# Modulation products of a two-block transformer kernel: from TensorE to accumulators on VectorE

## The reference

```python
cond_x = jax.nn.silu(c)
cond_c = jax.nn.silu(c_ctx)[None]
for i in range(DEPTH):
    sx1, cx1, gx1, sx2, cx2, gx2 = jnp.split((cond_x @ ada_w[i] + ada_b[i])[:, None, :], N_MOD, axis=-1)
    sc1, cc1, gc1, sc2, cc2, gc2 = jnp.split((cond_c @ ada_w[i] + ada_b[i])[:, None, :], N_MOD, axis=-1)
    hx = _modulate(_rms(x, norm_mix_g[i]), sx1, cx1)
    # layer 0: x = x + gx1 * mixer(hx), and the same for ctx with sc1, cc1, gc1
    # layer 1: attention; of the context only hc (sc1, cc1) is used
    x = x + gx2 * _mlp(_modulate(_rms(x, norm_mlp_g[i]), sx2, cx2), mlp_w1[i], mlp_w2[i])
    if not last:
        ctx = ctx + gc2 * _mlp(_modulate(_rms(ctx, norm_mlp_g[i]), sc2, cc2), mlp_w1[i], mlp_w2[i])
```

## Time and profile before

| | |
|---|---|
| median of three runs | 2355.6 us |
| the profiled execution, its own time | 2361.12 us |
| its span | 2359.3 us |
| TensorE busy | 2206.5 us, 94% |
| VectorE, ScalarE, GpSimd busy | 962.2, 786.0, 672.8 us |
| mean granted TensorE clock | 0.961 of full speed |
| moved by DMA | 199.92 MB |

### The profile page before, as it was taken

One profiled execution on the slowest core, in us unless ns is written; L12 is line 12 of the kernel. 1 busy time (PEld: TensorE's weight loads), 2 busy tenths in 40 slices (PEclk: granted clock), 3 DMA queues, 4 the chain that ended last, 5 costly groups with the idle time before them and its releaser, 6 DMA issues.

```text
span 2359.3 us, 33158 instructions
## 1 busy us (share of the span) xinstructions
PE 2206.5 (94%) x13714; PEld 1866.6 (79%) x13714; DVE 962.2 (41%) x1322; ACT 786.0 (33%) x1267; POOL 672.8 (29%) x314
## 2 busy tenths in 40 slices
PE   5999989999999998999899999999999896999987
PEld 3777877888888886789787788888898685977766
DVE  3223243222222225653592522222789324066662
ACT  2212223121221213432583422322323533255542
POOL 0321313222222221323495344444020123300002
PEclk9999989999999999999899999999999797999998
DMA  7443214213222231221223232323222010211111
GB/s 272 145 147 141 70 45 170 90 58 139 107 107 92 73 121 36 81 61 60 43 26 99 82 98 89 97 91 97 72 81 73 10 52 30 81 54 55 55 45 45
DMA packets 74313, 199.92 MB, mean 85 GB/s; under 512 B 24656, under 2 KB 25936, under 8 KB 74192
## 3 DMA queue, kind: packets, MB, share of 16 engines
q1 hardware_dynamic: 73008, 197.58, 25.8%
q10 hardware_dynamic: 1184, 0.61, 0.1%
HBM read 194.49 MB, written 2.10 MB: 83 GB/s over the span
## 4 chain that ended last, share of the span: by engine, by line
PE 86%; DVE 5%; POOL 3%; ACT 2%; issue 2%; DMA 1%; SPq 0%; DVEq 0%; ACTq 0%; POOLq 0%
PE ps L1990 60%; PE ps L2111 5%; PE ps L2471 5%; PE ps L2005 3%; POOL NAP L856 2%; PE ps L2040 2%; PE ps L2015 1%; PE ps L2029 1%; PE ps L2175 1%; PE ps L2093 1%; PE ps L2495 1%; PE ps L2022 1%; DVE S L1412 1%; DVE UC L1697 1%; POOL S L826 1%
## 5 line engine op out<-in xcount | busy, mean ns | idle before, releaser
L809 POOL TENSOR_TENSOR WL<-raw,WH 128x1024 fp32r<-128x1024 f32 x215 | 521.3, 2428 | 1390.8 <-ACT WH L906 1390.6
L906 ACT ACTIVATE WH<-raw 128x1024 fp32r<-128x1024 f32 x260 | 273.2, 1054 | 501.4 <-PE ps L1990 481.7
L1990 PE MATMUL ps<-HH,WH 128*128 128x512 f32 (+2 forms) x1568 | 428.1, 340 | 2.5 <-DVE HL L1799 2.5
L1990 PE MATMUL ps<-HL,WH 128*128 128x512 f32 (+2 forms) x1568 | 419.7, 334 | 0.0
L1990 PE MATMUL ps<-HH,WL 128*128 128x512 f32 (+2 forms) x1568 | 419.5, 334 | 0.0
L1990 PEld LDWEIGHTS ps<-HH,WH 128*128 128x128 f32 x1568 | 252.9, 189 | 62.3 <-issue 30.1
L1990 PEld LDWEIGHTS ps<-HL,WH 128*128 128x128 f32 x1568 | 252.2, 189 | 32.0 <-issue 1.4
L1990 PEld LDWEIGHTS ps<-HH,WL 128*128 128x128 f32 x1568 | 252.2, 189 | 31.2
L1990 PE MATMUL ps<-GH,WH 128*128 128x512 f32 (+1 forms) x896 | 267.9, 357 | 3.0 <-issue 3.0
L1990 PE MATMUL ps<-GL,WH 128*128 128x512 f32 (+1 forms) x896 | 268.1, 358 | 0.0
L1990 PE MATMUL ps<-GH,WL 128*128 128x512 f32 (+1 forms) x896 | 266.9, 356 | 0.0
(11 more groups left out here) (263 smaller groups left out, 3321.5 us busy)
## 6 DMA issues: line engine op xcount, KB each, us to landing
raw<-stream SPq DMA_DIRECT2D x260, 512.0 KB, 3.6
ring<-stream SPq DMA_DIRECT2D x40, 1024.0 KB, 4.9
ADA<-stream SPq DMA_DIRECT2D x4, 2048.0 KB, 20.3
XT<-rpb SPq DMA_DIRECT2D x128, 24.0 KB, 2.4
XT<-xT SPq DMA_DIRECT2D x1, 2048.0 KB, 8.7
out<-XT SPq DMA_DIRECT2D x8, 256.0 KB, 2.0
V1s<-V SPq DMA_DIRECT2D x6, 256.0 KB, 4.5
XT<-ctxT SPq DMA_DIRECT2D x1, 1024.0 KB, 11.3
```

The source lines that it names most:

```text
L809: nc.gpsimd.tensor_tensor(WL[:, slot, :], raw[:, slot, :], WH[:, slot, :].bitcast(F32), ALU.subtract).then_inc(lo_done[slot], 1)
L906: nc.scalar.activation(WH[:, slot, :], raw[:, slot, :], ACT.Copy).then_inc(hi_done[slot], 1)
L1990: ins = nc.tensor.matmul(pair(g)[:, cols], lhs, x[:, k, cols], start=first, stop=last)
```

## The change

The 20 later quads are computed on VectorE. Each weight tile is loaded alone (512 KB) into one of two slots (`tile_in`), 80 loads in place of 40. For each of its two blocks of inputs VectorE multiplies the 128 x 512 block with a per-partition scalar, the condition's value for that input, and adds it to an accumulator in SBUF (`ada_products`): two products a block in layer 0 and in the first four quads of layer 1 (`x` and the context), one in the other quads of layer 1, whose context modulation nobody reads. That is 256 products. Four accumulators of 512 columns are a batch. When a batch is complete, TensorE sums it over the partitions (`ada_sums`: two halves of four matmuls of 256 columns with `first`, 32 columns of which one is ones), VectorE copies the sums (`sums_out`), TensorE turns them (`ada_turn`, two halves of two narrow matmuls with `sel4`), and VectorE adds the bias (`ada_cols`). There are four batches in each layer: in layer 0 behind in1 4 and 11, after the first group of dft1, and behind out1 5; in layer 1 behind the second down projection of every other chunk; the turns stand one or two projections later. The two constants widen the constant table by 36 columns; `silu_c` and a clearing of `mod[1]` are new at the start.

```diff
+IN1_ADA = {1: 2, 2: 2, 3: 2, 4: 2, 5: 1, 6: 2, 7: 2, 8: 1, 9: 2, 11: 1, 12: 2, 13: 3, 14: 1, 15: 1}
+IN1_SUMS, IN1_TURNS = {4: 0, 11: 1}, {5: 0, 12: 1}
+    first = [(("in1", i), 0) for i, n in IN1_ADA.items() for _ in range(n)] + [(("out1", m), 0) for m in range(4) for _ in range(2)]
+    return first + [(("up", 0, c, i), c) for c in range(CHUNKS) for i in range(4) for _ in range(1 + c % 2)]
...
@@ SyncE
+            def load_weights(n):
+                if n == 0:
+                    sp.wait_ge(ada_rowed, 4)
+                if n >= 2:
+                    sp.wait_ge(acc_step, ada_tile(n - 1)[5])
+                if n == ADA_IN1:
+                    g = GROUP["dft1", 5]
+                    sp.wait_ge(ps_full[g % 4], turn(g) + 1)
+                layer, quad, kk = ada_tile(n)[0:3]
+                sp.dma_start(ada_ring(n), stream[TILE["ada", layer, 4 * quad + kk]]).then_inc(tile_in[n % 2], 16)
...
                 load_tile(n)
-                while pairs < len(ADA_PAIRS) and ADA_PAIRS[pairs][0] + 3 <= n:
+                while taken < len(ADA_TILES) and TILE[ADA_TILES[taken][0]] + 4 <= n:
+                    load_weights(taken)
...
@@ VectorE
+            nc.vector.tensor_tensor(silu_c[:], sig_c[:], v("cond"), ALU.mult).then_inc(silu_done, 1)
+            nc.vector.memset(mod[1][:], 0.0).then_inc(mod_zero, 1)
...
+            def ada_products(n, q=None):
+                layer, quad, kk, both, to, step = ada_tile(n)
+                count = 16 * (n // 2 + 1)
+                dve.wait_ge(tile_in[n % 2], count if q is None else count + 16 * 6 * q)
+                for k in (2 * kk, 2 * kk + 1):
+                    w = ada_ring(n)[:, 512 * (k % 2):512 * (k % 2) + 512]
+                    for x in range(1 + both):
+                        acc = (ada_acc0, ada_acc1)[n >= ADA_IN1][:, to + x, :]
+                        by = silu_c[:, 2 * k + x:2 * k + x + 1]
+                        if k == 0:
+                            ins = nc.vector.tensor_scalar(acc, w, by, None, ALU.mult)
+                        else:
+                            earlier = step - both
+                            dve.wait_ge(acc_step, earlier if q is None else earlier + 32 * q)
+                            ins = nc.vector.scalar_tensor_tensor(acc, w, by, acc, ALU.mult, ALU.add)
+                        ins.then_inc(acc_step, 1)
+                        step += 1
...
                     x_update(GROUP[kind, m], m, layer, 2, n, order=order)
+                    products_beside((kind, m))
+                    if kind == "out1" and m == 5:
+                        sums_out(0, 3)
+                    if kind == "out1" and m == 6:
+                        ada_cols(0, 3)
...
+                if i in IN1_TURNS:
+                    ada_cols(0, IN1_TURNS[i])
+                if i == 1:
+                    dve.wait_ge(silu_done, 1)
+                products_beside(("in1", i))
+                if i in (4, 10):
+                    sums_out(0, i // 10)
...
+                if t == 0:
+                    sums_out(0, 2)
...
+                        for j in range(1 + c % 2):
+                            ada_products(chunk_ada(c) + (1 + c % 2) * i + j, q)
...
@@ TensorE
-                    for quad, kk in ada_after_up(layer, c, i):
-                        if kk % 2:
-                            ada_pair(1, quad, kk // 2, q)
...
+            def ada_sums(layer, b, q=None):
+                steps = 32 * (b + 1) + 4 * ADA_0 * layer
+                acc = (ada_acc0, ada_acc1)[layer or b == 3]
+                for h in range(2):
+                    g = GROUP["adas", layer, b, h]
                     empty(g, q, MLP_G[0])
+                    pe.wait_ge(acc_step, steps if q is None else steps + 32 * q)
+                    for s in range(4):
+                        ins = nc.tensor.matmul(pair(g)[32 * s:32 * s + 32, 0:256], c_("first"), acc[:, s, 256 * h:256 * h + 256],
+                                               start=True, stop=True)
+                    ins.then_inc(ps_full[g % 4], 1)
...
+            def ada_turn(layer, b, q=None):
+                for h in range(2):
+                    g, rows = GROUP["adat", layer, b, h], GROUP["adas", layer, b, h]
                     empty(g, q, MLP_G[0])
+                    pe.wait_ge(ps_free[rows % 4], turn(rows, q, MLP_G[0]) + 1)
+                    for x in range(2):
+                        ins = nc.tensor.matmul(pair(g)[:, 4 * x:4 * x + 4], ada_rows[:, (2 * h + x) * P:(2 * h + x + 1) * P], c_("sel4"),
                                                start=True, stop=True)
...
+                    if layer == 0 and c % 2 == 0 and m == 1:
+                        ada_sums(1, c // 2, q)
+                    if layer == 0 and c % 2 == 0 and m == 3:
+                        ada_turn(1, c // 2, q)
```

More of the change, by code:

```diff
@@ L168, in norm, with sums, turns @@
         g(("norm", r))
+    def sums(layer, b):
+        for h in range(2):
+            g(("adas", layer, b, h))
+    def turns(layer, b):
+        for h in range(2):
+            g(("adat", layer, b, h))
     g(("adaf", 0))
@@ L175, in _groups @@
             g(("adaf", 1))
[L176 to L180, removed]
+        if i in IN1_SUMS:
+            sums(0, IN1_SUMS[i])
+        if i in IN1_TURNS:
+            turns(0, IN1_TURNS[i])
     for t in range(6):
         g(("dft1", t))
-    g(("adat", 0, 2))
+        if t == 0:
+            sums(0, 2)
+    turns(0, 2)
     for j in range(4):
@@ L187, in _groups @@
         g(("out1", m))
+        if m == 5:
+            sums(0, 3)
+        if m == 6:
+            turns(0, 3)
     def up(layer, c):
@@ L198, in down @@
             g(("down", layer, c, m))
-            if layer == 0 and c % 2 == 0 and m == ADA_TURN:
-                g(("adat", 1, c // 2))
+            if layer == 0 and c % 2 == 0 and m == 1:
+                sums(1, c // 2)
+            if layer == 0 and c % 2 == 0 and m == 3:
+                turns(1, c // 2)
     def mlp(layer):
@@ new lines, in products_beside, with sums_out @@
+            def products_beside(tile):
+                for n in range(ADA_0):
+                    if ADA_TILES[n][0] == tile:
+                        ada_products(n)
+            def sums_out(layer, b, q=None):
+                for h in range(2):
+                    g = GROUP["adas", layer, b, h]
+                    full(g, q, MLP_G[0])
+                    nc.vector.tensor_scalar(ada_rows[:, 256 * h:256 * h + 256], pair(g)[:, 0:256], 1.0, None, ALU.mult)\
+                      .then_inc(ps_free[g % 4], 1)
@@ L1608, in mlp_down @@
                     x_update(GROUP["down", layer, c, m], m, layer, 5, MLP_N[layer], q, MLP_G[layer])
-                    if layer == 0 and c % 2 == 0 and m == ADA_TURN:
+                    if layer == 0 and c % 2 == 0 and m == 1:
+                        sums_out(1, c // 2, q)
+                    if layer == 0 and c % 2 == 0 and m == 3:
                         ada_cols(1, c // 2, q)
```

162 lines of the change are left out of this document (69 added, 93 removed).

## The result

The changed kernel takes 2318.07 us (median of four runs, 2317.63 to 2320.05), the kernel before on the same chip 2355.24 us (2354.24 to 2362.46): a ratio of 0.9836, 95% interval 0.9823 to 0.9848, some 37 us or 1.6% less. The profiled executions are 2361.12 and 2320.05 us, 41.1 apart; their spans are 2359.3 and 2318.3.

A forecast was written before the change was run, and what follows sets the result against it. TensorE, busy 94% of the span, was taken to bound in1 and the layer-0 MLP. Savings of 3 up to dft2, -3 in out1 and 29.6 in the MLP sum to 29.6 us off 2355.6: 2326, range 2309 to 2342.

The forecast's parts named there:

- (a): Whole kernel: the port costs VectorE 2.4 us a tile, two waits in in1, TensorE saved in the MLP; 2326 us, chance 0.70.
- (b): Whole kernel: VectorE keeps up, its products slipping between GpSimd's cycles; 2311 us, chance 0.14.
- TensorE work that goes: In1, dft1 and MLP: 40 pairs at 1.17 us, turns at 3.67 or 2.57, slow clock of 1.4 to 1.5 after some.
- TensorE work that comes: Eight batches of sums and turns on TensorE, each 3.0 us (2.1 to 4.8).
- VectorE's products: 256 products of 512 columns on VectorE, 0.68 to 0.77 us each by columns; a tile of four 2.7.
- The port's cost: VectorE beside GpSimd: a product stands still for a whole GpSimd instruction of 2.40 us, up to 3.1 instead of 0.7.
- The first wait: In1, sums after projection 4: TensorE waits 12.5 us for batch 0, 14 with 1.4 for the clock.
- The second wait: Sums after the first dft1 group: TensorE waits 7 us behind 46 us of VectorE work; dft2 starts 22 after in1.
- Out1: Out1: one batch more on TensorE, -3.0 us; no wait, 5 us if loads are slow.
- The MLP's cover: Layer-0 MLP: VectorE's work in an up step, 8.4 us, only just fits the step's 8.43; yield 29.6.
- (c): Whole kernel: slow clock of 1.4 us after each of eight batches, and loads at 5 us; centre 2340 us, chance 0.10.
- (d): MLP: VectorE becomes the bound there too, from about 8.9 us per up step; kernel at 2370 us, chance 0.06.

The follow-up runs named there:

- 64-column kernel: The changed kernel with each matmul of the sums taking 64 of its 256 columns: 2315.62 us, one run.
- one-group kernel: The changed kernel with all four matmuls of a half of the sums writing to partitions 0 to 31: 2342.71 us, one run.
- ring of three: The changed kernel with three slots instead of two for the weight tiles of in1: 2309.85 us, ratio 0.9801 to the kernel before.
- the kernel with one-column products: The changed kernel with its 224 accumulating products cut to one column, loads, waits and order kept: 2299.22 us, ratio 0.9746 to the kernel before.
- short GpSimd work: The changed kernel with GpSimd's subtraction writing one column instead of 1024 for tiles from in1 4 to out1: 2303.60 us, ratio 0.9765.

## Why the prediction was right, and where its terms were off

The forecast, 2326, was case (a), and its mechanism is the one measured: TensorE is saved in the MLP, and two waits appear in in1 and dft1. The time alone does not say so: 2318 is 8 us from (a)'s 2326 and 7 from (b)'s 2311. The waits of 9.10 and 7.72 us do, where (b) had 0 to 1 and 3.6, and so do products of up to 2.96 us. The median gain, 37.2, is 7.6 us above the forecast's 29.6. Between the two profiled spans it is 41.0, 11.4 above: 5.7 in the MLP, 3.2 up to dft2, 0.2 in out1, and 2.2 behind the MLP, which no term covers.

1. **TensorE work that goes** (pairs at 1.17, turns at 2.57, a slow clock after some) was about right. A round of the MLP now is 16 x 8.41 (126.11 / 15) + a batch; before it was 145.6 in the mean of the three distances, of which 134.5 are projections too, and 11.1 modulation. The terms had 6 x 1.17 + 2.57 + 0.7 = 10.3. Of the other 0.8, 0.3 are slow stretches (1.55 and 1.53 us behind two of these three turns, 1.0 a round) and 0.2 are pairs, which cost 1.20 by the projections of 8.41 that are left; 0.3 a round I leave open.

2. **TensorE work that comes is the term that was off**: 3.0 us a batch. Measured are 136.50 - 134.5 = 2.0, of which 1.00 the sums, 0.79 the turn. The prediction had both ends, 0.5 a half by halving the row with 512 columns and 0.84 by the weight loads in line, and took the latter. The 64-column kernel shows that loads of 32 columns set nothing here, and the one-group kernel why. Eight batches are 8 us; four of them make the MLP's yield 33.6 instead of 29.6 (measured 35.3).

3. **VectorE's products.** 0.68 to 0.77 us each was forecast from the convolution; measured are 0.742 for one and 0.66 from one to the next in a run, a tile of four 2.73 (2.7). The port's cost was forecast as one GpSimd instruction of 2.4 in full for each that it meets, 3.1 us for such a product. The longest took 2.96: up to 2.2 us are lost, and less where the product would have waited for its load anyway. The Trainium skill states a lock of this kind in "SBUF — State Buffer", section "Who interferes with whom": the pair of ports that VectorE shares with GpSimd goes to one instruction at a time, and the order of issue decides who blocks. The trace agrees where the starts lie apart: a product begun 0.12 us ahead of GpSimd kept its 0.74 and the subtraction took 2.88 (128.38, below), one begun behind takes up to 2.92. Where both begin within 0.02 us, as in most up steps of the MLP, it is the product that waits each time; in the ring of three a subtraction that began 0.03 us ahead (127.30) lost and took 7.13. Starts so near do not tell who wins.

```profile
128.38 2.88 POOL L809 TENSOR_TENSOR WL<-raw,WH 128x1024 fp32r<-128x1024 f32 x1 [8.64 <-ACT WH L906]
```

4. **The first wait**, forecast 12.5, was 9.10. Batch 0 was forecast to take 40.6 us (20.4 of products, 16.2 stolen, 4 bare for loads) and took 36.9: 20.2 of products (six tiles at 2.66 from one to the next, two at 2.12), 3.0 bare, and 13.5 stolen. The block of four GpSimd instructions stole 8.3 in place of 9: the first four products and the block take 10.4 us together. The three lone instructions stole 1.1, 2.0 and 2.1 in place of 7.2, the first of them so little because VectorE stood waiting for a load when it began (81.07; the product begins at 82.17). TensorE was there at 95.99, 0.5 us earlier than forecast. The sums at 1.94 and the projection at 9.08 add 1.4, as forecast for the clock.

5. **The second wait**, forecast 7 after 46 us of VectorE's work from the end of in1 11, was 7.72 after 45.0 (167.41 to 212.43). What was missed stands behind it: the clock is at 0.50 there too, the 40 records of the dft1 groups take 10.23 (five groups at 1.75 were forecast, 8.75), and dft2 starts 24.6 us after in1, not 22. Up to dft2 the sum was 2.5 (rounded to 3): two batches add 2.0, the shorter wait 3.4, the later dft2 takes 2.6, and pairs and start add some 0.8. That makes 6.1, measured 6.2.

6. **Out1** -2.8 (forecast -3.0), near by luck. The batch itself is 1.8 (1.00 + 0.79). Another 1.4 is the first projection: TensorE stands idle for 2.96 us before it in both kernels, but behind that the clock is at 0.50 for some 5.5 us here (up to 254.5), where it was low for some 3 us before, and the projection takes 11.3 (53.30 - 5 x 8.40) in place of 9.9. Why the clock comes back later here is not shown. There is no wait for products.

7. **The MLP's cover** was called just enough (8.4 of 8.43 us), and it held: no TensorE wait, no slip, and the kernel with one-column products is no faster there. Once VectorE has caught up (from 386 us on) a step takes it 6.3 to 7.25 us, with the 0.95 before it up to 8.2 of 8.40. The estimate was 0.2 too high.

**The rivals.** (b), products slipping between GpSimd's cycles at no cost, is wrong as a rule, though with the ring of three a run of 14 products passed at no cost to VectorE; short GpSimd work shows what it would have been worth, 2304 for the kernel. (c), a clock fall behind every batch: none behind the turns in in1, out1 and the MLP; it fell in the two waits, where the prediction had it for the first only. (d), VectorE as the bound of the MLP: no sign.

## What to carry to other kernels

Work moved to another engine costs nothing only where that engine gets it done before its result is asked for, so check that step by step. The place where the result is asked for is a free choice: here one projection later took the ratio from 0.9836 to 0.9787, where a third buffer gave 0.9801 and nearly free products 0.9746. Find who needs the result before you fix where it is waited for. Where the nearest rows give two prices for a small matmul, look at which part of the array each one uses. Price a shared port by its meetings: a product lost what was left of the GpSimd instruction it met, 2.2 us at most, and nothing while VectorE would have waited for a load anyway; a GpSimd instruction can lose a whole run of products. And when two terms miss in opposite directions, as in out1, a stretch that comes out right proves neither.

## What the runs showed of the hardware that I had not expected

- Four fp32 matmuls with 32 columns of weights, each to its own 32 partitions, 256 columns: 0.50 us together, 1.79 in one group; with 64 columns 0.18.
- A VectorE multiply of one strided fp32 input (every second element) takes 479 ns for 512 columns, and it too stands for a GpSimd instruction (up to 2695 ns).
- While GpSimd runs back to back (10.32 us for four), VectorE gets one instruction in after each of its instructions. The other way round it need not: in the ring of three a GpSimd subtraction waited through a run of 14 products and took 11.49 us in place of 2.4.
- Narrow matmuls of 0.79 us leave the granted clock at 1.00 where other matmuls follow at once; the same kind for 2.58 us lets it fall to 0.50 to 0.60 for about 4 us behind four of the eight turns.
- Behind a wait of 2.4 us the clock fell in one kernel (next projection 10.01) and not in another (8.60).
